# Gate and up projections of a two-block decoder kernel: 512-column chunks taken in pairs over seven PSUM banks, with two of the eight k-tile pairs by Strassen's seven block products

## The reference, cut to what matters

```
h2 = rms_norm(x, g_ffn)                                       # (256, 2048)
x  = x + (jax.nn.silu(h2 @ w_gate) * (h2 @ w_up)) @ w_down    # w_gate, w_up: (2048, 5632), w_down: (5632, 2048)
```

## Time and profile before

| | |
|---|---|
| three executions, median (lowest to highest) | 2788.55 us (2788.11 to 2788.79) |
| profiled execution, first to last instruction (its span) | 2785.8 us |
| outside the span, against the median | 2.75 us |
| TensorE busy | 2771.9 us, 99% of the span |
| VectorE busy | 1497.6 us, 54% |
| ScalarE busy | 1227.7 us, 44% |
| granted TensorE clock, mean | 0.999 |

### The profile page before, as it was taken

How to read it: one execution, slowest core, us unless ns; L and a number is a source line. 1 busy time by engine, 2 the same in 40 slices (tenths; PEclk the granted TensorE clock), 3 DMA queues, 4 the chain that set the end, 5 groups by cost and what they waited for, 6 DMA issues and landing times.

```text
span 2785.8 us, 30416 instructions
## 1 busy us (share of the span) xinstructions
PE 2771.9 (99%) x13185; PEld 2308.9 (83%) x13185; DVE 1497.6 (54%) x1215; ACT 1227.7 (44%) x1293; POOL 14.8 (1%) x28
## 2 busy tenths in 40 slices
PE   9999999999999999999999999999999999999999
PEld 7888778888888888888888888888888888888887
DVE  5445764455465445455455684665555455544555
ACT  5335664345554343343444545344433333333453
POOL 0000000000000000000000000000000000000000
PEclk9999999999999999999999999999999999999999
DMA  7645036555455655655556654555655555556555
GB/s 234 219 146 166 31 121 204 191 193 198 166 181 187 193 194 182 196 184 194 186 191 206 200 183 152 180 161 183 215 186 195 190 189 188 190 195 196 173 183 174
DMA packets 256437, 508.15 MB, mean 182 GB/s; under 512 B 8162, under 2 KB 18992, under 8 KB 255408
## 3 DMA queue, kind: packets, MB, share of 16 engines
q1 hardware_dynamic: 254112, 495.61, 54.5%
q0 software_dynamic: 2016, 10.36, 1.1%
q10 hardware_dynamic: 176, 0.23, 0.0%
HBM read 504.08 MB, written 2.10 MB: 182 GB/s over the span
## 4 chain that ended last, share of the span: by engine, by line
PE 87%; ACT 0%; DVE 0%; issue 0%
PE acc L683 27%; PE acc L684 27%; PE acc L688 27%; PE tb L669 2%; PE acc L949 0%; PE tb L1000 0%; ACT prob L1579 0%; PE acc L891 0%; PE acc L888 0%; PE acc L890 0%; PE tb L965 0%; PE tb L1167 0%; PE tb L1177 0%; PE tb L1196 0%; PE tb L1217 0%; PE acc L928 0%
## 5 line engine op out<-in xcount | busy, mean ns | idle before, releaser
L1853 DVE TENSOR_TENSOR wlo<-raw,whi 128x2048 fp32r<-128x2048 f32 (+1 forms) x465 | 1063.8, 2289 | 863.0 <-ACT whi L1349 862.2
L1349 ACT ACTIVATE whi<-raw 128x2048 fp32r<-128x2048 f32 (+1 forms) x465 | 889.3, 1914 | 985.4 <-PE acc L688 786.3
L683 PE MATMUL acc<-whi,ahi 128*128 128x512 f32 (+1 forms) x1968 | 767.8, 391 | 0.4 <-DVE alo L1945 0.4
L684 PE MATMUL acc<-whi,alo 128*128 128x512 f32 (+1 forms) x1968 | 762.2, 388 | 0.0
L683 PE MATMUL acc<-whi,bhi 128*128 128x512 f32 x1528 | 597.6, 391 | 0.0
L684 PE MATMUL acc<-whi,blo 128*128 128x512 f32 x1528 | 595.2, 390 | 0.0
L688 PE MATMUL acc<-wlo,ahi 128*128 128x512 f32 (+1 forms) x1968 | 484.4, 388 | 0.0
L683 PEld LDWEIGHTS acc<-whi,ahi 128*128 128x128 f32 x1968 | 370.2, 188 | 75.7 <-DVE wlo L1942 0.9
L684 PEld LDWEIGHTS acc<-whi,alo 128*128 128x128 f32 x1968 | 370.6, 188 | 73.2
L688 PEld LDWEIGHTS acc<-wlo,ahi 128*128 128x128 f32 x1968 | 367.3, 188 | 75.3
L688 PE MATMUL acc<-wlo,bhi 128*128 128x512 f32 x1528 | 378.0, 390 | 0.0
(11 more groups left out here) (339 smaller groups left out, 1540.9 us busy)
## 6 DMA issues: line engine op xcount, KB each, us to landing
raw<-in_w_ff SPq DMA_DIRECT2D x128, 1024.0 KB, 5.2
raw<-in_w_in SPq DMA_DIRECT2D x119, 1024.0 KB, 5.1
raw<-in_w_gate SPq DMA_DIRECT2D x44, 1024.0 KB, 5.2
raw<-in_w_up SPq DMA_DIRECT2D x44, 1024.0 KB, 5.2
raw<-in_w_down SPq DMA_DIRECT2D x44, 1024.0 KB, 5.1
raw<-in_w_out SPq DMA_DIRECT2D x16, 1024.0 KB, 5.1
raw<-in_w_o SPq DMA_DIRECT2D x16, 1024.0 KB, 5.1
raw<-in_w_ple_gate SPq DMA_DIRECT2D x16, 1024.0 KB, 5.2
```

Source lines behind the costliest of these rows:

```text
L683: nc.tensor.matmul(out_(t), hi[:, kt, tt(t)], whi[:, slot, wc(k)], start=first and k == 0, stop=False)
L684: nc.tensor.matmul(out_(t), lo[:, kt, tt(t)], whi[:, slot, wc(k)], start=False, stop=False)
L1349: nc.scalar.activation(whi[:, g % SPLIT, 0:n_], raw[:, g % RAW, 0:n_], ACT.Copy).then_inc(w_hi, 1)
L1853: V.tensor_tensor(wlo[:, g % SPLIT, 0:n_], raw[:, g % RAW, 0:n_], whi[:, g % SPLIT, 0:n_].bitcast(F32), ALU.subtract).then_inc(w_lo, 1)
```

## The change

Write A1, A2 for the two k-tiles of a step (for two token tiles each) and the gate and up columns as the two column blocks. A step is one 1 MB load of two k-tiles of both weights, so a double chunk has eight steps. A direct step ("D") makes the 8 block products of a 2x2 by 2x2 block product, 24 matmuls, as before. A Strassen step ("S") makes 7, 21 matmuls, from sums of activation tiles and sums of weight blocks. The plan is `DDSDDSDD`.

- **Items.** An S step is two items in the `whi`/`wlo` ring: "B" (three blocks as loaded, 9 matmuls) and "T" (four blocks that VectorE adds up, 12 matmuls). Ten items for eight loads. With items numbered 0 to 9, items 2, 3 and 6, 7 are the S steps, and 10, 11 are the next double chunk's 0 and 1.
- **Loads.** Each load of these is two transfers of 512 KB, one of `w_up` and one of `w_gate`. A `raw` slot with sums is free at the second count of `t_sum`.
- **Sums.** `weight_sums` on VectorE writes `tsum` (in the place of `wlo`) once TensorE is through with the item three before, then `sums_hi` on ScalarE and two subtractions.
- **Banks.** Seven results are accumulated: `b2`, `q6`, `q7`, `q3` in `acc0` and `acc1`, `q5`, `q4` in `tb0`, `b1` in half of `tb1`. The other half, `turn_bank`, takes the transposes, four at a time.
- **The end of a double chunk.** VectorE combines the banks (`e0`, `e1`, `e2`, `e0` again); the first of these frees the bank in which the next double chunk starts. ScalarE makes two SiLUs, VectorE two products.
- **Tiles.** The sums of activation tiles are made once, while the last chunks of `w_o_2` run.

```diff
+GUD_PLAN = "DDSDDSDD"
+NTILE = {"D": 6, "S": 7}
+STEP_ITEM = [n + GUD_PLAN[:n].count("S") for n in range(len(GUD_PLAN) + 1)]
+DC_ITEMS = STEP_ITEM[-1]
...
# SP
+                    if KINDS[g] == "T":
+                        sp.wait_ge(t_sum, 2 * SUMS_BEFORE[g] + 2)
+                    else:
+                        sp.wait_ge(w_lo, g + 1)
...
+                for f, src in enumerate((src2, src1)):
+                    sp.dma_start(into[:, :, f, :], src[:, 2 * step:2 * step + 2, c:c + COLS]
+                                 ).then_inc(raw_in[n % RAW], 16)
...
# TensorE: first and last step of a double chunk
+                    parts = ((b2, 0, 1), (q3, 4, 0), (q5, 2, 0), (q4, 2, 1))
+                    if begin:
+                        pe.wait_ge(w_lo, w.val("group", 1))
...
+                            if begin and n == 0:
+                                pe.wait_ge(acc_free[c % 2], c // 2)
+                            elif begin and n == 1:
+                                pe.wait_ge(acc_free[(c + 1) % 2], (c + 1) // 2)
+                            elif begin and d:
+                                pe.wait_ge(q_free, 2 * d + n - 3)
...
+                            if end and n < 3:
+                                mm.then_inc(bank_done, 1)
...
# TensorE: an S step
+                    products7(((b1, at, 0, start, stop), (b2, at + 1, 2, False, False),
+                               (q3, at + 6, 1, False, False)), slot, n)
...
+                    products7(((q5, at + 3, 0, False, False), (q7, at + 5, 1, start, stop),
+                               (q6, at + 4, 2, start, stop), (q4, at + 2, 3, False, False)), slot, n)
...
# ScalarE
+            def sums_hi(g):
+                for n in range(2):
+                    act.wait_ge(t_sum, 2 * SUMS_BEFORE[g] + 1 + n)
+                    part = slice(2 * n * COLS, 2 * (n + 1) * COLS)
+                    nc.scalar.activation(whi[:, g % SPLIT, part], tsum[:, g % SPLIT, part], ACT.Copy
...
+                block_of(DC_ITEMS, hooks | {DC_ITEMS - 1: first_sum})
...
+                nc.scalar.activation(e0[:, 0, :], e0[:, 0, :], ACT.Silu, scale=nrs[:, 0:1]).then_inc(silu_done, 1)
+                act.wait_ge(q_free, 2 * d + 2)
+                nc.scalar.activation(e0[:, 1, :], e0[:, 1, :], ACT.Silu, scale=rstd[:, R_FFN2, 1:2]
...
# VectorE
+            def weight_sums(g):
+                dve.wait_ge(mm_done, g + 1 - SPLIT)
+                V.tensor_tensor(v2(t[:, 0:2 * COLS]), both(r[:, 0:COLS]), v2(r[:, COLS:3 * COLS]), ALU.add
+                                ).then_inc(t_sum, 1)
+                dve.wait_ge(t_sum, 2 * n + 1)
+                link(V.tensor_tensor(t[:, col(2)], t[:, col(0)], r[:, col(2)], ALU.add))
+                linked()
+                V.tensor_tensor(t[:, col(3)], t[:, col(2)], r[:, col(3)], ALU.add).then_inc(t_sum, 1)
...
+                block_of(DC_ITEMS, hooks)
...
+                dve.wait_ge(s1_out, d + 1)
+                dve.wait_ge(bank_done, 3 * d + 1)
+                V.tensor_tensor(e0[:, :, :], v2(x[:, :]), both(s1[:, :]), ALU.add).then_inc(free_x, 1)
...
+                V.tensor_tensor(e1[:, :, :], v2(y[:, :]), both(e0[:, 1, :]), ALU.add).then_inc(free_y, 1)
...
+                    half = lambda k: (lambda: turn(ahi, alo, 4 * (n - 1) + 2 * k, 2, src=turn_bank))
+                    hooks = {STEP_ITEM[4]: half(0), STEP_ITEM[6]: half(1)} if n else {}
```

More of the change, by code:

```diff
@@ L141, in __init__ @@
     def __init__(self):
-        self.n = dict(group=0, chunk=0, turn=0, link=0, used=0, hid=0, gate=0)
+        self.n = dict(group=0, chunk=0, turn=0, link=0, used=0, hid=0, gate=0, double=0, built=0)
     def val(self, name, off=0, div=1, mul=1):
@@ L190, in plan_items, with item_kinds, load_of, landed @@
     return items, (range(0, len(items)),)
+G_GUD = 319
+GUD_PLAN = "DDSDDSDD"
+GUD_PAIRS = (4, 4, 3)
+NTILE = {"D": 6, "S": 7}
+TILE_AT = [sum(NTILE[k] for k in GUD_PLAN[:n]) for n in range(len(GUD_PLAN) + 1)]
+TILES = TILE_AT[-1]
+STEP_ITEM = [n + GUD_PLAN[:n].count("S") for n in range(len(GUD_PLAN) + 1)]
+DC_ITEMS = STEP_ITEM[-1]
+FIRST_S, LAST_S = GUD_PLAN.index("S"), GUD_PLAN.rindex("S")
+def item_kinds():
+    kinds, twice = ["W"] * G_GUD, [False] * G_GUD
+    for pairs in GUD_PAIRS:
+        one = [k for step in GUD_PLAN for k in (("B", "T") if step == "S" else ("W",))]
+        kinds += one * pairs + ["W"] * 4 * pairs
+        twice += [True] * len(one) * pairs + [False] * 4 * pairs
+    return kinds + ["W"] * 18, twice + [False] * 18
+KINDS, TWICE = item_kinds()
+SUMS_BEFORE = [KINDS[:g].count("T") for g in range(len(KINDS) + 1)]
+ITEMS_OF = [[g for g in (n, n + 1) if g == n or g < len(KINDS) and KINDS[g] == "T"]
+            for n in range(len(KINDS)) if KINDS[n] != "T"]
+def load_of(g):
+    return g - SUMS_BEFORE[g] - (KINDS[g] == "T")
+def landed(n):
+    return 16 * sum(1 + TWICE[ITEMS_OF[m][0]] for m in range(n % RAW, n + 1, RAW))
 DHEAD = {"nsa": DK, "mla": NOPE + ROPE}
@@ L592, in gud @@
                 for c in range(pairs):
-                    chunks(wg, b * 4 * COLS + (c - 4) * COLS, 0)
-                    chunks(wu, b * 4 * COLS + (c - 4) * COLS, 0)
+                    for step in range(len(GUD_PLAN)):
+                        load_pair(wg, wu, b * 4 * COLS + (c - 4) * COLS, step)
                 for c in range(4):
@@ L1274, in _, with half_turn @@
                 chunk(ahi, alo, hook=lambda n=n: turn_chunk(h, n - 1, C_O2 + n - 1), head=(xhi, xlo))
[L1277 to L1281, removed]
+            def half_turn(srcs, *waits):
+                for wait in waits:
+                    pe.wait_ge(*wait)
+                pe.wait_ge(turned, w.val("turn"))
+                for n, src in enumerate(srcs):
+                    last = nc.tensor.transpose(turn_bank[:, n * P:(n + 1) * P], src, ident)
+                last.then_inc(turn_ready, 1)
+                w.n["turn"] += 1
@@ new lines, in hid2, with turn_hid2, with_hi @@
+            def hid2(c0, n=GKT):
+                return [e2[:, 1 - t, c0 + k * P:c0 + (k + 1) * P] for k in range(n) for t in range(TT)]
+            def turn_hid2(half):
+                half_turn(hid2(half * 2 * P, 2), (hid2_ready, w.val("double")))
+            def with_hi(o, tile, slot, quad, start=False):
+                nc.tensor.matmul(o, fhi[:, tile, :], whi[:, slot, col(quad)], start=start, stop=False)
+                nc.tensor.matmul(o, flo[:, tile, :], whi[:, slot, col(quad)], start=False, stop=False)
@@ new lines, in with_lo, with double_chunk, direct, products7 @@
+            def with_lo(o, tile, slot, quad, stop=False):
+                return nc.tensor.matmul(o, fhi[:, tile, :], wlo[:, slot, col(quad)], start=False, stop=stop)
+            def double_chunk(hooks={}, need={}):
+                c, d = w.n["chunk"], w.n["double"]
+                x, y = acc[c % 2], acc[(c + 1) % 2]
+                b2, q6, q7, q3 = x[:, 0:COLS], x[:, COLS:], y[:, 0:COLS], y[:, COLS:]
+                q5, q4, b1 = tb[0][:, 0:COLS], tb[0][:, COLS:], tb[1][:, 0:COLS]
+                def direct(at, slot, begin, end):
+                    parts = ((b2, 0, 1), (q3, 4, 0), (q5, 2, 0), (q4, 2, 1))
+                    if begin:
+                        pe.wait_ge(w_lo, w.val("group", 1))
+                        pe.wait_ge(turned, w.val("turn"))
+                    if begin or end:
+                        for n, (o, tile, half) in enumerate(parts):
+                            if begin and n == 0:
[4 more added lines that the diff above has]
+                                pe.wait_ge(q_free, 2 * d + n - 3)
+                            for k in range(2):
+                                with_hi(o, at + tile + k, slot, 2 * k + half, begin and k == 0)
+                                if end and n == 0 and k == 0:
+                                    pe.wait_ge(w_lo, w.val("group", 1))
+                                mm = with_lo(o, at + tile + k, slot, 2 * k + half, end and k == 1)
+                            if end and n < 3:
+                                mm.then_inc(bank_done, 1)
+                    else:
+                        for o, tile, half in parts:
+                            for k in range(2):
+                                with_hi(o, at + tile + k, slot, 2 * k + half)
+                        pe.wait_ge(w_lo, w.val("group", 1))
+                        for o, tile, half in parts:
+                            for k in range(2):
+                                mm = with_lo(o, at + tile + k, slot, 2 * k + half)
+                    mm.then_inc(mm_done, 1)
+                    w.n["group"] += 1
+                def products7(parts, slot, n):
+                    for o, tile, quad, start, stop in parts:
+                        with_hi(o, tile, slot, quad, start)
+                    pe.wait_ge(w_lo, w.val("group", 1))
+                    for o, tile, quad, start, stop in parts:
+                        mm = with_lo(o, tile, slot, quad, stop)
+                    mm.then_inc(mm_done, 1)
```

(45 more changed lines are left out.)

177 lines of the change are left out of this document (138 added, 39 removed).

## The result

The changed kernel takes 2851.55 us (median of 4 runs, 2850.35 to 2855.02) against 2788.51 for the kernel before (4 runs): a ratio of 1.023, 95% interval 1.0215 to 1.0244. It is 63 us slower; 41 were forecast. That is outside the forecast's own range of 2816 to 2844 and inside the wider one of 2802 to 2858, which was drawn to take in a fall of the clock.

What follows compares the result with a forecast made beforehand. TensorE, busy for 99% of the span, was taken as the bound. Eleven stalls of 4.4 us less 15.0 saved give +33.8; with +4 and +3 that is +41, so 2829 us, own range 2816 to 2844.

Steps and rivals of the forecast that it cites:

- e0: VectorE's first combination of the banks at a double chunk's end, 128x1024 from PSUM: 1.30 us with hand-overs.
- the wider one: Range of 2802 to 2858 us, from a stall of 2.6 up to the slow clock and late sums.
- What is removed: On TensorE, 186 matmuls instead of 192 per double chunk; 66 fewer over eleven, saving 15.0 us.
- The chain to the first combination: From item 1's end through conversions and loads to VectorE's first combination: 36.6 us against TensorE's 32.2, stalling 4.4 per double chunk.
- step 2: Load of items 6 and 7, its copies, subtractions and sums until its `raw` slot is free: 11.85 us.
- this sign: In the changed kernel's trace, ends of double chunks should stand 47.5 to 48 us apart.
- +4 for the first double chunk: Last tile sums on ScalarE and VectorE delay the first double chunk: +4 us, between 0 and 10.
- +3 for two transfers: Gate/up loads as two 512 KB transfers: 0.1 us for each of 33 chain loads, +3, at most 12.2.
- The clock: Rival: TensorE's clock falls after each of 11 stalls, adding 18 us, 2847 in all; chance 0.14.
- the rule quoted there: Trainium skill's statement that gaps between bursts of matmuls bring TensorE's clock down; no size given.
- Late sums: Rival: slower sums make TensorE wait inside item 7 too, +20 us, 2849 in all; chance 0.08.
- Rival of a keeping ring: Weight ring keeps up, first combination done before the last matmul, the 15 us simply saved: 2773.6 us; chance 0.10.

Runs made afterwards that it cites:

- banks first, DDSDSDDD: Changed kernel with the four bank combinations before item 11's conversion and the second S step one place earlier; 2775.26 us, ratio 0.9955 to the kernel before.
- the filler: Changed kernel with 14 unused matmuls of 512 columns where TensorE waits at the end of each double chunk; 2825.71 us, ratio 1.0136 to the kernel before.
- Banks first: Changed kernel with the four bank combinations before item 11's conversion on VectorE, plan kept; 2784.42 us, ratio 0.9988 to the kernel before.
- the plan alone: Changed kernel with plan DDSDSDDD, banks still combined behind item 11; 2838.81 us, ratio 1.0185 to the kernel before.
- one S step: Changed kernel with plan DDSDDDDD, 33 matmuls saved instead of 66, banks still combined behind item 11; 2805.75 us, ratio 1.0064 to the kernel before.
- half loads: Changed kernel with each gate/up transfer bringing one k-tile instead of two, so output is not the reference's; 2792.26 us (one run).

## Why the prediction was right, and where it was off

- *What is removed, 15.0 us.* Right. Where nothing waits, 13.1 us of it arrive (banks first, DDSDSDDD).
- *The chain to the first combination, 36.6 us from the end of item 1.* Right, with its steps: 4.54, 11.95, 9.43, 9.51 and 1.26 make 36.7. (The terms of step 2 add up to 11.88 and not 11.85, which changes nothing.) The stall was priced at 4.4 and is 4.3 on average over 11. Undoing the order takes 44.5 us of waiting away, shorter loads take 36 away. A double chunk was to take 47.5 to 48 us: with the filler, at full clock, those behind the first take 47.0 to 47.8. In the changed kernel itself the slow stretches make it 50.3 (2053.42 to 2103.74); there this sign did not come.
- *+4 for the first double chunk.* Right in kind, some 2.5 in size: in the filler's trace the first takes 50.0 us and the others 47.0 to 47.8.
- *+3 for two transfers.* Nothing of it shows. The pair lands as one did: the second lands a median of 4.7 after its own issue, which comes 0.41 behind the first, 5.1 in all against 5.2. The 2.0 us a transfer that the prediction quotes are, by the title of their section, for transfers that GpSimd issues. SP issues these, and nothing like 66 us appears.
- *All of it at full clock.* The filler's profiled span is 39.6 us longer than before. 2.3 of that are there before the first gate/up matmul (1952.09 against 1949.81), which leaves 37.3 where 41 were forecast. The 2.3 are no part of the change. At about 185 us, where no instruction is changed, the clock stays low for longer in the changed kernel's trace and in the filler's than in that of before: a mean of 0.50 from 182 to 192 us in both against 0.83, which is 10 x 0.33 = 3.3 us. The length of this stretch varies from trace to trace (the best kernel's is as short as that of before), so differences of a few us between single traces mean little.
- *The clock.* This is the step that failed. The forecast's own sum has the clock's fall at nothing and leaves it to a rival with a chance of 0.14, but it happened at all eleven ends. Without it the time would have been in the forecast's own range: the filler's 2825.7 is. And its price, 18 us, was too low: the filler measures 26. I took each stretch as long as the one in rows 8; of the eleven, five are 3.4 us and six 6.8. The time of that case, 2847, with 8 more for the longer stretches, is 2855; measured are 2851.6. That this lies in the wide range is owed to the rival, not to the forecast. That no wait of this length was in the trace of before was a reason not to know, and I read it as a reason to doubt; the rule quoted there deserved more than half of the chance.
- *Late sums.* Did not come: sums with a broadcast operand take 1.22 us for 1024 columns, as the nearest row.
- *Rival of a keeping ring.* It needed a chain under 32.2 us. Banks first take item 11 out of it, and by the prediction's terms 36.6 less the last turn of 9.47 leaves 27.1; 2.9 us of waits are left there.

## What to carry to other kernels

On engines that work in strict order, list for every buffer that is handed back what stands ahead of the hand-back, and follow that back through its own loads and slots: here a conversion for the next chunk, with three turns of a two-slot ring behind it, held up 4.3 us of an engine that was busy for 99%. A saving on the bound engine pays only as far as the ring behind it has time in hand (here 1.4 us for each two loads), and of the plans run here those did best that put the extra work on the slot that does not lead to the next hand-over. That alone was worth only 13 us while the order stood: engines that work in order pass a delay from one slot to the other. Price a new stall of TensorE with the slow clock behind it, not by its length alone.

## What the runs showed of the hardware

The changed kernel's eleven waits (up to 5.4 us) were all followed by the lower clock, for 3.4 or 6.8 us each; of the somewhat shorter eleven with the plan alone (2.9 to 5.3) ten were. With 3.2 us of idle matmuls put into the same gaps, which left waits of up to 1.4 us, it never fell there. Of the eleven waits of the kernel with one S step (up to 2.4 us) two were followed by it, and so were two of the eleven with half loads (up to 2.7). No length parts the two kinds: a wait of 3.3 us with the plan alone was not followed by the lower clock, and one of 2.2 with one S step was.

The best kernel (banks first, DDSDSDDD), span and mean granted clock, the clock as before:

```profile
core 0: 2772.7 us, clock 0.999
```

Two transfers of 512 KB issued 0.41 us apart had both landed 5.1 us after the first issue; one of 1024 KB took 5.2.
